# Two unread 128x512 products per slot, at the end of each slot of the recurrence stage

## The reference

```python
def step(S, inp):
    w_t, k_t, v_t, kk_t, kka_t = inp[:5]
    S = (S * w_t[:, :, None, :]
         - jnp.einsum('bhij,bhj->bhi', S, kk_t)[..., None] * kka_t[:, :, None, :]
         + v_t[..., None] * k_t[:, :, None, :])
    y = jnp.einsum('bhij,bhj->bhi', S, inp[5]) if emit else None
    return S, y
...
y = rwkv_readout(ys[0] + ys[1], r, dirs[0][1] + dirs[1][1], v, g, r_k, ln_g, ln_b, wo, h.dtype)
```

## Time and profile before

| | us |
|---|---|
| median of 3 runs | 4894.6 |
| lowest and highest | 4889.67, 4904.01 |
| the profiled execution | 4903.26 |
| its span | 4901.4 |
| mean granted TensorE clock | 0.955 of full speed |
| the recurrence stage in it, from the first L1462 to the end of slot 23 | 1445 to 2231, so 786 |

### The profile page before, as it was taken

The page is one execution under the profiler, slowest core; times in us unless marked ns, Lnnn a source line. Parts: engine busy times, 40 slices in busy tenths (PEclk is TensorE's granted clock), DMA queues, the critical chain, the costliest instruction groups (busy, mean ns, idle before and its releaser), DMA issues.

```text
span 4901.4 us, 70197 instructions
## 1 busy us (share of the span) xinstructions
PE 4668.6 (95%) x29914; PEld 3306.4 (67%) x29914; DVE 2702.3 (55%) x4820; ACT 1038.8 (21%) x2331; POOL 81.2 (2%) x81
## 2 busy tenths in 40 slices
PE   8999999998988999899999999999999999989998
PEld 5556555555546666675788588744888788645886
DVE  3162445525335666663555566674656756674656
ACT  1052000002025555552000201043001110152000
POOL 0000000000000000000000000020000000020000
PEclk9998999998988898899999999989999999989999
DMA  5211222211100000002122222210222212211221
GB/s 233 103 44 52 80 109 104 103 69 52 64 1 2 3 3 2 2 37 78 69 86 86 74 89 82 95 69 35 88 90 89 86 69 82 99 52 56 93 92 44
DMA packets 27045, 339.09 MB, mean 69 GB/s; under 512 B 3024, under 2 KB 3024, under 8 KB 6896
## 3 DMA queue, kind: packets, MB, share of 16 engines
q1 hardware_dynamic: 24048, 324.51, 17.6%
q0 software_dynamic: 2688, 10.09, 0.6%
HBM read 330.40 MB, written 4.19 MB: 68 GB/s over the span
## 4 chain that ended last, share of the span: by engine, by line
PE 88%; DVE 6%; ACT 4%; issue 2%; DMA 0%; SPq 0%; DVEq 0%; ACTq 0%
PE ps L1348 45%; PE ps L1066 23%; PE ps L1541 2%; PE ps L1138 2%; PE ps L1472 2%; PE ps L1513 1%; PE ps L1524 1%; PE ps L1603 1%; PE ps L1108 1%; PE ps L1462 1%; PE ps L1590 1%; PE ps L1587 1%; ACT arena L1781 1%; PE ps L1289 1%; PE ps L1416 1%
## 5 line engine op out<-in xcount | busy, mean ns | idle before, releaser
L1348 PE MATMUL ps<-arena 128*128 128x256 f32 (+1 forms) x9096 | 2111.9, 394 | 15.1 <-DVE arena L2605 15.1
L1348 PEld LDWEIGHTS ps<-arena 128*128 128x128 f32 x9096 | 1734.3, 191 | 380.5 <-DVE arena L2605 17.5
L1066 PE MATMUL ps<-arena 128*128 128x512 f32 (+3 forms) x3104 | 1150.3, 532 | 10.8 <-ACT arena L1732 7.5
L1066 PEld LDWEIGHTS ps<-arena 128*128 128x128 f32 x3104 | 584.5, 192 | 565.5 <-issue 400.0
L2596 DVE TENSOR_TENSOR arena<-ps,arena 128x512 f32<-128x512 f32 (+1 forms) x250 | 157.6, 630 | 314.8 <-PE ps L1348 313.0
L2596 DVE TENSOR_TENSOR square<-ps,square 128x512 f32<-128x512 f32 (+1 forms) x145 | 99.2, 684 | 175.4 <-PE ps L1348 175.3
L2537 DVE TENSOR_TENSOR arena<-arena 128x1024 f32<-128x1024 f32 (+2 forms) x153 | 190.5, 1245 | 8.7 <-ACT arena L1732 5.4
L1922 ACT COPY square<-ps 128x512 f32<-128x512 f32 (+1 forms) x65 | 37.2, 573 | 659.4 <-PE ps L1348 592.3
L2852 DVE COPY_PREDICATED arena<-const,ps 128x256 f32<-128x256 int32 x192 | 83.8, 444 | 115.7 <-PE ps L1541 111.9
L2011 ACT COPY arena<-ps 128x256 f32<-128x256 f32 x240 | 87.8, 371 | 259.9 <-PE ps L1513 259.6
L1541 PE MATMUL ps<-arena 64*64 64x64 f32 x3072 | 130.0, 227 | 12.8 <-ACT arena L1993 12.2
(11 more groups left out here) (341 smaller groups left out, 4991.9 us busy)
## 6 DMA issues: line engine op xcount, KB each, us to landing
arena<-in_panels SPq DMA_DIRECT2D x144, 2048.0 KB, 7.8
arena<-in_panels SPq DMA_DIRECT2D x9, 1536.0 KB, 6.4
arena<-in_bias POOLq DMA_DIRECT2D x8, 512.0 KB, 4.6
arena<-in_x_in SPq DMA_DIRECT2D x1, 3072.0 KB, 10.7
x_save<-arena POOLq DMA_DIRECT2D x1, 2048.0 KB, 7.5
arena<-x_save POOLq DMA_DIRECT2D x1, 2048.0 KB, 12.9
out_x<-arena SPq DMA_DIRECT2D x8, 256.0 KB, 2.2
arena<-in_panels SPq DMA_DIRECT2D x1, 1792.0 KB, 11.6
```

The costliest lines, as they stand in the source:

```text
L1066: ins = pe.matmul(dest, left(k), right(k), start=(k == 0), stop=(k == nk - 1))
L1348: ins = pe.matmul(bank[:, j * cut.side:(j + 1) * cut.side], left[:, k, j * P:(j + 1) * P], right[k], start=(k == 0), stop=(k == cut.rows - 1))
```

## The change

In each slot t = 0 to 23, after `prep` of direction 1 in steps k = 13 and k = 15, PE issues one more product: the 128x128 identity by 512 columns of V, into the next shared bank. It signals nothing and nobody reads it. In readout slots the gate's product, in step 14, lies between the two. No other engine gets an instruction. Since the products take a turn in the banks, misc_banks hands out others behind them: in readout slots the gate goes to the other bank, and the waits for free banks at the start of the next slot change places.

```diff
+        WARM_AT = (13, 15)
...
                     if t < groups:
                         e["prep"](t, 1, k)
+                    if t < groups and k in WARM_AT:
+                        e["warm"](t, k)
                     for what, d, i in FEATURES[t % GROUPS].get(k, ()):
...
+            def warm(t, k):
+                b = len(plan) % 2
+                plan[("warm", t, k)] = (4 + b, last[b])
...
+            def warm(t, k):
+
+                pe.matmul(ps[:, misc("warm", t, k), :], ident, V[:, 0, 0:COLS], start=True, stop=True)
```

More of the change, by code:

```diff
@@ L788, in readout @@
                     use((what, p), signal, p + 1)
+            def warm(t, k):
+                b = len(plan) % 2
+                plan[("warm", t, k)] = (4 + b, last[b])
             skip = lambda *a: None
-            rwkv_steps(dict(prep=prep, scan=skip, feature=feature, readout=readout, fill=skip))
+            rwkv_steps(dict(prep=prep, scan=skip, feature=feature, readout=readout, fill=skip, warm=warm))
             return plan
@@ L972, in _ @@
             model(dict(load=load, mod=mod, gains=skip, norm_mod=skip, even_in=even_in, attention=skip, project=project,
-                       post=skip, mlp=mlp, odd_in=odd_in, prep=skip, scan=skip, feature=skip, readout=skip, fill=skip, odd_out=odd_out, enter=skip, swiglu=swiglu, final=skip,
+                       post=skip, mlp=mlp, odd_in=odd_in, prep=skip, scan=skip, feature=skip, readout=skip, fill=skip, warm=skip, odd_out=odd_out, enter=skip, swiglu=swiglu, final=skip,
                        mix_in=mix_in, conv=skip, store=store))
@@ L1039, in _ @@
             model(dict(load=load, mod=mod, gains=skip, norm_mod=skip, even_in=even_in, attention=attention, project=skip,
-                       post=skip, mlp=skip, odd_in=odd_in, prep=skip, scan=skip, feature=skip, readout=skip, fill=skip, odd_out=odd_out, enter=skip, swiglu=swiglu, final=skip,
+                       post=skip, mlp=skip, odd_in=odd_in, prep=skip, scan=skip, feature=skip, readout=skip, fill=skip, warm=skip, odd_out=odd_out, enter=skip, swiglu=swiglu, final=skip,
                        mix_in=conv_taps, conv=skip, store=skip))
@@ L1671, in _ @@
             model(dict(load=load, mod=mod, gains=skip, norm_mod=norm_mod, even_in=even_in, attention=attention,
-                       project=project, post=post, mlp=mlp, odd_in=odd_in, prep=prep, scan=scan, feature=feature, readout=readout, fill=fill, odd_out=skip, swiglu=swiglu, enter=skip, final=final, mix_in=mix_in, conv=skip, store=skip))
+                       project=project, post=post, mlp=mlp, odd_in=odd_in, prep=prep, scan=scan, feature=feature, readout=readout, fill=fill, warm=warm, odd_out=skip, swiglu=swiglu, enter=skip, final=final, mix_in=mix_in, conv=skip, store=skip))
         @block.scalar
@@ L2115, in _ @@
             model(dict(load=load, mod=mod, gains=skip, norm_mod=norm_mod, even_in=even_in, attention=attention,
-                       project=project, post=post, mlp=mlp, odd_in=odd_in, prep=prep, scan=scan, feature=feature, readout=readout, fill=skip, odd_out=skip, swiglu=swiglu,
+                       project=project, post=post, mlp=mlp, odd_in=odd_in, prep=prep, scan=scan, feature=feature, readout=readout, fill=skip, warm=skip, odd_out=skip, swiglu=swiglu,
                        enter=enter, final=skip, mix_in=mix_in, conv=conv, store=skip))
@@ L3083, in _ @@
             model(dict(load=load, mod=mod, gains=gains, norm_mod=norm_mod, even_in=even_in, attention=attention,
-                       project=project, post=post, mlp=mlp, odd_in=odd_in, prep=prep, scan=scan, feature=feature, readout=readout, fill=skip, odd_out=skip,
+                       project=project, post=post, mlp=mlp, odd_in=odd_in, prep=prep, scan=scan, feature=feature, readout=readout, fill=skip, warm=skip, odd_out=skip,
                        swiglu=swiglu, enter=enter, final=final, mix_in=mix_in, conv=conv, store=skip))
```

## The result

The changed kernel takes 4910.52 us (median of 20 runs, 4905.12 to 4924.19) against 4900.82 us before (20 runs). The ratio is 1.0021 with a 95% interval of 1.0014 to 1.0029: some 10 us slower, less than the 0.3% that the chances speak of, but clear of the measurement. I had forecast a draw, 0.6 us faster than the median then known. The time lies inside the range; the sign of the small move was wrong.

The account below looks back on a forecast made before the run. PE sets the pace almost everywhere, with 86 us of full clock missing. Costs 40.6 us less gains of 25.8, 14 and 1 us give -0.2 us, carried to the median as 4894 us; range 4875 to 4914 us.

Parts of the forecast that it names:

- the product of step 15 in context slots: End of each context slot: no cover, priced at 1.05 us like every step 15 product, 25.2 us over all 24 slots.
- the price at full clock: Each added product on PE: 1.05 us to the next start, with 0.96 us kept for the range.
- Falls at the starts of context slots: Behind plain slots: all six low-clock starts (slots 3, 6, 12, 15, 18, 21) go, saving 4.3 us each, 25.8 us.
- their 14.8 us: Plain slots: cost of both products, 1.05 us for step 15 and 0.8 us for step 13, in each.
- an edge nearly reached: Start of slot 9: the same small work alone once did not bring the clock down, so all six falls taken as gone.
- Falls behind context slots: Starts of slots after context slots: low clock costs 23 us, stays likely but shorter; 0.6 saved, 14 us, bounds nothing to 23.
- my 1.85: A plain slot: 1.05 us for the step 15 product plus 0.8 us for step 13, which hides one wait.
- the cover of the product of step 13 in context slots: In seven of eight context slots its 1.05 us vanishes in PE's 2.81 us wait for ACT; without cover, 7.4 us return.
- the waits for banks: At the new products and the next slot's start: earlier readers have finished with the banks, so cost nothing.
- The rule on idle gaps: Ties clock falls to idle gaps between product bursts; slot 6 should not have started slow; prediction followed the trace instead.
- The slower rival: Starts of context slots: low clock stays, all 40.6 us paid plus 5.7 us, 4941 us; chance 0.15.

Follow-up runs that it names:

- e5: Changed kernel without the product of step 15 in context slots, all others kept; ratio 0.9995 to the kernel before.
- e2: Kernel before plus the products of steps 13 and 15 in context and readout slots, none in plain slots; ratio 0.9994.
- e1: Kernel before plus the products of steps 13 and 15 in the eight plain slots alone; ratio 0.9980.
- e4: Kernel before plus one product in step 14 of plain slots and two in step 14 of context slots, inside PE's wait; ratio 0.9939.
- e3: Kernel before plus one product in step 14 of plain slots only, amid the small blocks; ratio 0.9955.
- e7: Kernel before plus the products of steps 13 and 15 in readout slots alone; ratio 0.9996, median 4896.08 us.
- e9: Changed kernel without either product in context slots, those in readout and plain slots kept; ratio 0.9986 to the kernel before.
- e6: Kernel before plus the products of steps 13 and 15 in plain slots and of step 15 in context slots; ratio 0.9986.
- e10: Kernel before plus two products in step 14 of context slots, inside PE's 2.8 us wait, none elsewhere; ratio 0.9979.
- e11: Kernel before plus two products in step 14 of context slots and one in step 8 of readout slots, all inside waits; ratio 0.9980.
- e12: Kernel before plus two products once, in step 3 of slot 2, shifting later slots about 2 us; ratio 0.9999, median 4900.81 us.

## Why the prediction was wrong

By kind of slot, the sum of the prediction and the profiled executions of both kernels:

| slots | forecast, us | measured, us |
|---|---|---|
| context (0, 3, ... 21) | 8.4 + 0.8 - 25.8 = -16.6 | 318.97 to 310.62: -8.4 |
| plain (2, 5, ... 23) | +14.8 | 213.63 to 226.98: +13.3 |
| readout, and slot 1 | 16.6 - 14 - 1 = +1.6 | 253.23 to 257.76: +4.5 |
| the stage | -0.2 | +9.5 |

- **The step that failed: the product of step 15 in context slots.** I took 1.05 us, the price at full clock, while the same text said that a fall remains likely just there. It takes 2.01 us in seven of the eight slots of the profiled execution, all but slot 21, which is 6.7 us more. Taking these eight products away moved the ratio from 1.0021 to 0.9995 (e5), 13 us and more than the whole loss, so this term is enough to turn the sign. Taking away the products in plain slots turns it as well (e2), but their price was right. The mis-sized term is not all: without the term my sum would have been -0.2 - 8.4 = -8.6 us, and e5 stands at -2.5 us (-6.9 to +1.5).
- **Put at nothing: falls in places that had none.** In the profiled execution one of 13.65 us in the midst of slot 3 makes it 45.95 us against 39.45 us for its like, 6.5 us; one of 6.83 us in slot 13 makes it 1.9 us longer than slot 7; and in slots 17 and 20 a short one, shown for slot 17 (2046.99), lies right over the product of step 15, which takes 1.8 us there. The one in slot 3 also comes in the profiles of e1 and e4, each of them the slowest execution of its kernel, and not in those of e2, e3 and e7. The changed kernel's profiled execution was faster than its median with it, so the loss of 10 us does not need it.
- **Luck the other way**: slot 0 took 38.71 us and not 41.79, though it holds one of the products of 2.0 us, since a stretch of 17 us at half clock in its midst was missing this time (its clock is 0.81 where it was 0.66, rows at the end of this section). With 6.7 us for the price and 6.5 for slot 3, these 5 us leave the context slots about 8 us behind the forecast. That the time fell into the range is owed to its width, not to the sum.
- **Falls at the starts of context slots**: they went, as forecast, and at the forecast size: slot 6 gained 2.2 us net of its product of 2.0. But the reason that I gave is wrong. I credited the products in plain slots by what stands around a start, and e2 and e7 are rid of the falls with nothing in plain slots. Beside the other products, those in plain slots therefore cost their 14.8 us for nothing: from e2 to the change the time goes from 0.9994 to 1.0021, 13 us. The rows ahead of the prediction had the hint: slot 9 escaped with the same work around it, and I read that as an edge nearly reached and not as a matter of when the work comes.
- **Terms that do not add**: e1 and e2 stand at -10 and -3 us and their union at +10. I had priced each edit as if it moved only its own stretch. This did not enter the total of this one change, in which the 25.8 us stand once, but it hid that e1's third of the products does better than all of them.
- **Falls behind context slots**: right in kind, 6.83 us where three of them had lasted 10.24, but the readout slots took 2.9 us more than forecast, about 2 of them by the new fall in slot 13.
- **Right**: the price at full clock, 1.06 us measured, and 1.81 us for two in a plain slot against my 1.85; the cover of the product of step 13 in context slots, which take 37.45 us with it and 37.44 without (e5, e9); the waits for banks, since no wait stands at L1616 or at the L1470 behind it.
- **The rule on idle gaps** that the prediction cites from the Trainium skill, "TensorE: Matmul & The Clock Gate", section "Why this matters for your kernels", did not decide here: the clock fell at the starts of context slots without such a gap, and filling 1.9 of the 2.8 us of a wait (e4) shortened the fall behind it and did not end it.
- **The slower rival** (falls stay) did not happen: the clock of the stage rose to 0.95. So the loss is not from falls that stayed.

Slot 0 before, then in the changed kernel:

```profile
1445.22:1487.01 41.79, 36.37 (x464) 25.33 (x464) 18.50 (x32) 23.16 (x46) 0.00 (x0) 0.66 0.01 2
```

```profile
1441.60:1480.31 38.71, 32.63 (x469) 22.38 (x469) 19.71 (x35) 24.43 (x50) 0.00 (x0) 0.81 0.01 2
```

Of the causes, the price of the step 15 products is shown by their rows and by e5; the weight of the falls in new places is read from one execution. What makes rounds hold near 95.5 and 99.0 us is not shown by these runs, and neither is what brings a fall at a given start. That rounds of six kernels with different products (e1, e6, e7, e9, e10, e11) took 99.0 to 99.2 us is, and that the cost of one more product hangs on the others.

## What to carry to other kernels

Where PE's clock switches in a repeated pattern, the unit to measure is the whole round, not the product: price it at the clock that holds at its place, and time candidates together, since their gains can be one and the same gain. Put such products where PE waits anyway (two of them in a wait of 2.8 us cost nothing and made the slot 0.8 us shorter), and one amid the small products instead of one at either side (0.9955 against 0.9980). The wait alone was not enough here (e10, 0.9979). The version with both (e4) is 0.61% faster than the kernel before and 0.82% faster than the changed one.

## What the runs showed of the hardware

- The granted clock fell to 0.5 behind products of 32x32 blocks and the small ones of scan, with no wait over 0.22 us among them, and not only after long waits: the start of slot 6 before.
- The same work in the same order, within one execution, started a slot at 1.0 or at 0.5: slots 6 and 9 of e12, 37.45 and 41.79 us.
- A 128x128 by 128x512 float32 product is two matrix instructions and takes 1.06 us to the next start at full clock and 2.01 us at half; in another place 0.96 us at full clock (1674.72 to 1675.68).
- Unread products of about 1.8 (e1), 2.1 (e7) and 4 us (e9) a round all gave rounds of 99.0 to 99.2 us. The time at half clock differs between them: from the start of slot 6 to the end of slot 7 it is 13.7 us in e1 and in e7 and 6.8 us in e9.
